# Expert rows gated on GpSimd, and added to x by accumulating transfers

## The reference

```python
sh1, sc1, gt1, sh2, sc2, gt2 = ada_mod(cond, lp['w_ada'], lp['b_ada'])   # cond: c for latent, c_ctx for context tokens
...
h2 = rms_norm(x, lp['norm2_g']) * (1.0 + sc2) + sh2
x = x + gt2 * hier_moe(h2, lp)      # 16 experts (1024 -> 512 -> 1024), two for each token, weights in combine
...
y = rms_norm(x, final_g)
```

## Time and profile before

| | us |
|---|---|
| median of 3 runs | 749.33 |
| lowest and highest | 747.24, 749.91 |
| the profiled execution, its own time | 750.44 |
| its span | 748.7 |
| busy: TensorE, VectorE | 704.5 (94%), 534.5 (71%) |
| busy: ScalarE, GpSimd | 411.4 (55%), 109.7 (15%) |

### The profile page before, as it was taken

How to read it: one execution, slowest core, us unless ns; L and a number is a source line. 1 busy time by engine, 2 the same in 40 slices (tenths; PEclk the granted TensorE clock), 3 DMA queues, 4 the chain that set the end, 5 groups by cost and what they waited for, 6 DMA issues and landing times.

```text
span 748.7 us, 10728 instructions
## 1 busy us (share of the span) xinstructions
PE 704.5 (94%) x3842; PEld 533.3 (71%) x3842; DVE 534.5 (71%) x837; ACT 411.4 (55%) x623; POOL 109.7 (15%) x166
## 2 busy tenths in 40 slices
PE   6699999989999999999999289999999999999994
PEld 2268898949977895555544278888888888888863
DVE  4363616289632035666656889999999999999997
ACT  4762532241232134545543467888888888778933
POOL 3000000000031027654221101111111111111000
PEclk9999999999999999999999589999999999999998
DMA  8991135032389609900029888999999999999663
GB/s 324 415 394 44 60 165 197 1 132 108 142 200 291 240 17 383 264 2 29 6 97 350 277 322 303 362 371 380 374 380 401 376 386 399 354 389 394 238 242 144
DMA packets 81506, 186.26 MB, mean 249 GB/s; under 512 B 9156, under 2 KB 19684, under 8 KB 78260
## 3 DMA queue, kind: packets, MB, share of 16 engines
q1 hardware_dynamic: 73252, 166.64, 60.9%
q0 software_dynamic: 6448, 16.86, 6.6%
q10 hardware_dynamic: 1760, 2.17, 1.0%
HBM read 173.16 MB, written 18.38 MB: 256 GB/s over the span
## 4 chain that ended last, share of the span: by engine, by line
PE 84%; DVE 7%; DMA 4%; ACT 2%; issue 1%; SPq 1%; POOLq 0%; DVEq 0%; ACTq 0%
PE bank L2072 56%; PE bank L1965 13%; PE bank L1974 6%; DMA slot<-in_w_ada 4%; PE bank L1985 2%; PE bank L2234 2%; PE bank L2212 1%; PE bank L2205 1%; DVE WL L1769 1%; PE bank L2035 1%; DVE big L1903 1%; DVE big L1913 1%; DVE big L1908 1%; DVE big L1843 1%; SPq L654 1%
## 5 line engine op out<-in xcount | busy, mean ns | idle before, releaser
L1769 DVE TENSOR_TENSOR WL<-slot,WH 128x1024 fp32r<-128x1024 f32 x188 | 219.2, 1220 | 9.5 <-ACT WH L1222 8.4
L1222 ACT CAST WH<-slot 128x1024 fp32r<-128x1024 f32 x188 | 183.4, 1057 | 1.4 <-PE bank L2072 1.4
L2072 PE MATMUL bank<-WH,xgTh 128*128 128x512 f32 x256 | 102.4, 400 | 3.1 <-DVE xgTl L1761 3.1
L2072 PE MATMUL bank<-WH,xgTl 128*128 128x512 f32 x256 | 100.7, 393 | 0.0
L2072 PE MATMUL bank<-hTh,WP 128*128 128x384 f32 (+1 forms) x320 | 100.0, 312 | 0.0
L2072 PE MATMUL bank<-hTh,WL 128*128 128x384 f32 (+1 forms) x320 | 98.7, 308 | 0.0
L2072 PE MATMUL bank<-hTl,WP 128*128 128x384 f32 (+1 forms) x320 | 98.7, 308 | 0.0
L2072 PE MATMUL bank<-WL,xgTh 128*128 128x512 f32 x248 | 96.5, 389 | 0.0
L1965 PE MATMUL bank<-slot,big 128*128 128x512 f32 (+1 forms) x224 | 87.7, 539 | 0.1
L1974 PE MATMUL bank<-ident,big 128*128 128x128 f32 x424 | 60.7, 284 | 7.0 <-DMA big<-h_scratch,big 5.1
L1965 PEld LDWEIGHTS bank<-slot,big 128*128 128x128 f32 x224 | 40.9, 190 | 35.1 <-issue 33.1
(11 more groups left out here) (283 smaller groups left out, 1076.5 us busy)
## 6 DMA issues: line engine op xcount, KB each, us to landing
slot<-in_w_down SPq DMA_DIRECT2D x16, 2048.0 KB, 16.7
slot<-in_w_up SPq DMA_DIRECT2D x15, 2048.0 KB, 17.7
slot<-in_w_gate SPq DMA_DIRECT2D x13, 2048.0 KB, 17.6
slot<-in_w_ada SPq DMA_DIRECT2D x12, 2048.0 KB, 11.1
slot<-in_w_in SPq DMA_DIRECT2D x6, 2048.0 KB, 22.4
y_scratch<-dftp SPq DMA_DIRECT2D x1, 5120.0 KB, 35.7
big<-y_scratch SPq DMA_DIRECT2D x10, 512.0 KB, 7.4
slot<-in_w_out SPq DMA_DIRECT2D x2, 2048.0 KB, 15.1
```

The costliest lines, as they stand in the source:

```text
L1222: act.copy(WH[:, high_half(w, s), r, :], quarter(n, s, w, r)).then_inc(high_ok[w], 1)
L1769: dve.tensor_tensor(quarter_low(n, s, w, r), quarter(n, s, w, r), WH[:, high_half(w, s), r, :].bitcast(F32), ALU.subtract).then_inc(low_ok ...
L2072: ins = pe.matmul(out, l[u], r[v], start=first and i == 0, stop=last and i == 2)
```

## The change

Six edits:

1. **GpSimd gates rows ahead of the scatter.** `gate_of` builds, for each of the 128 slots of an expert, its gate row: two comparisons of the token number with 511.5, then in two halves of 512 columns context gate x side, latent gate x side, and their sum. `scatter` multiplies the expert's 128 x 1024 results by it. Step m is now gate_of(m - 1), gather(m + 2), scatter(m - 1).
2. **The last two experts** get their gate rows behind the last scatter (`last_gate`). VectorE multiplies their banks by them (`last_gated`); `kept_high` copies that, `kept_low` subtracts.
3. **Accumulating transfers.** SP's ten loads go. GpSimd issues five transfers that add the first table to x in SBUF, then, each behind its own tile's first, five that add the second.
4. **The end.** TensorE's identity products go; it runs the last rows of slot 0 for tiles 0 to 2, then slot 1's, then tiles 3 and 4. VectorE adds the two banks to x and norms.
5. **x is kept.** SP stores x to `x1_scratch`, five transfers of 512 KB (for the branch that isn't taken): three ahead of the first expert weights, one behind gt2, one ahead of the load of expert 2's up weights.
6. **Places.** `fg` moves to the end of the loop, `gate_row` takes its place; VectorE's `keep_rows` copies two columns instead of one.

```diff
-SUM_BANKS = [(2, 3), (4, 7), (5, 6), (2, 3), (4, 7)]
+SUM_BANKS = [(2, 3), (4, 7), (5, 6), (0, 1), (2, 3)]
+SUMS_AHEAD = 3
...
+            for b in range(NT - 2):
+                sp.wait_ge(wt2_ok, ADDED[("wa", b, 1)])
+                keep_x1(b)
             full(sp, "o", NT - 2)
...
+            sp.wait_ge(x1_ok, 2)
+            keep_x1(NT - 1)
             load_weights(1, 2, 0, 1)
...
-            def load_results():
-                table = y_dram.rearrange("(k t p) n -> p t k n", k=2, p=P)
-                for t in range(NT):
-                    for k in range(2):
-                        sp.dma_start(yab[:, t, k], table[:, t, k]).then_inc(yab_in[t][k], 16)
...
-            def scatter(n, s):
+            def gate_rows(n, tokens, out):
+
+                for c, op in enumerate((ALU.is_lt, ALU.is_gt)):
+                    ins = pool.tensor_scalar(side[:, c:c + 1], tokens, LAT - 0.5, None, op)
+                ins.then_inc(side_ok, 1)
+                pool.wait_ge(side_ok, n + 1)
+                pool.sem_inc(gather_go, 1)
+                for h in range(2):
+                    half = slice(h * 512, (h + 1) * 512)
+                    if h == 1:
+                        pool.wait_ge(gate_ok, 2 * n + 1)
+                        pool.sem_inc(gather_go, 1)
+                    pool.tensor_scalar(other_gate, gt2[:, 1, half], side[:, 1:2], None, ALU.mult)
+                    pool.tensor_scalar(out[:, half], gt2[:, 0, half], side[:, 0:1], None, ALU.mult).then_inc(gate_part, 1)
+                    pool.wait_ge(gate_part, 2 * n + h + 1)
+                    pool.sem_inc(gather_go, 1)
+                    pool.tensor_tensor(out[:, half], out[:, half], other_gate, ALU.add).then_inc(gate_ok, 1)
+
+            def gate_of(n, s):
 
                 pool.wait_ge(sidx_ok, n + 1)
+                wait_past(pool, y_gated, n)
+                pool.sem_inc(gather_go, 1)
+                gate_rows(n, kept_rows[:, s, 0:1], gate_row)
+
+            def scatter(n, s, gated=True):
+
                 pool.wait_ge(y_cp, n + 1)
+                if gated:
+                    pool.wait_ge(gate_ok, 2 * n + 2)
+                    pool.sem_inc(gather_go, 1)
+                    pool.tensor_tensor(yout[:, s, :], yout[:, s, :], gate_row, ALU.mult).then_inc(y_gated, 1)
...
+                if m != 0 and not kept(p, m):
+                    gate_of(n - 1, 1 - s)
                 if m is None or m + 2 < NE:
                     gather(n + 2, s)
                 if m != 0 and not kept(p, m):
                     scatter(n - 1, 1 - s)
+
+            def add_results(again):
+
+                table = y_dram.rearrange("(k t p) n -> p k t n", k=2, p=P)
+                for t in range(NT):
+                    pool.dma_start(x[:, t, :], table[:, 0, t], accum_op=ALU.add).then_inc(results_added[t], 16)
+                for t in range(NT):
+                    pool.wait_ge(results_added[t], 32 * again + 16)
+                    pool.dma_start(x[:, t, :], table[:, 1, t], accum_op=ALU.add).then_inc(results_added[t], 16)
             pool.wait_ge(table_zero, 16)
             one_pass(0)
+            pool.wait_ge(used[0], (NE - 1) * 4)
+            pool.wait_ge(idx_ok, NE)
+            for s in range(KEPT):
+                gate_rows(NE - KEPT + s, idx[:, s, 0:1], last_gate[:, s, :])
+            pool.wait_ge(x1_out, 16 * NT)
+            for s in range(2):
+                pool.wait_ge(y_out[s], (pairs - 1) * 16)
+            add_results(0)
...
+                    act.wait_ge(last_y_ok, 2 * s + h + 1)
+                    act.copy(yH[s][:, h * 512:(h + 1) * 512], last_y[s][:, h * 512:(h + 1) * 512]).then_inc(yH_ok, 1)
...
+                    last_gated(0)
+                    selection(1)
                     kept_low(0)
-                    selection(1)
-                    for t in range(NT - 1):
-                        both_results(t)
+                    last_gated(1)
                     kept_low(1)
...
+                    dve.scalar_tensor_tensor(out=last_y[s][:, half], in0=kept_bank(s, h), scalar=1.0 / W_SCALE,
+                                             in1=last_gate[:, s, half], op0=ALU.mult, op1=ALU.mult).then_inc(last_y_ok, 1)
...
             def added(t, again):
+                dve.wait_ge(results_added[t], 32 * again + 32)
                 for h in range(2):
                     half = slice(h * 512, (h + 1) * 512)
                     dve.wait_ge(f_sum, 2 * (again * NT + t) + h + 1)
+                    dve.tensor_tensor(x[:, t, half], x[:, t, half], bank[SUM_BANKS[t][h]][:, :], ALU.add).then_inc(x_final, 1)
...
             def final(again):
                 for t in range(NT):
-                    gated(t, again)
                     added(t, again)
-                    if t == 0 and again == 0:
-                        both_results(NT - 1)
-                    elif t > 0:
+                    if t > 0:
                         final_norm(t - 1, again)
                 final_norm(NT - 1, again)
...
+                pe.wait_ge(last_y_ok, 2)
+                for s in range(KEPT):
+                    for t in range(SUMS_AHEAD):
+                        rows_added(t, s)
+                for t in range(SUMS_AHEAD, NT):
+                    if t == SUMS_AHEAD:
+                        pe.wait_ge(last_y_ok, 2 * KEPT)
+                    else:
+                        pe.wait_ge(x_final, 2 * (again * NT) + 2)
                     for s in range(KEPT):
+                        rows_added(t, s)
```

More of the change, by code:

```diff
@@ L929, in _ @@
                 for t in range(NT):
-                    for k in range(2):
-                        pool.wait_ge(yab_in[t][k], 16)
+                    pool.wait_ge(results_added[t], 32)
                 pool.wait_ge(f_sum, 2 * NT)
                 for s in range(2):
-                    scatter(NE - 2 + s, s)
+                    scatter(NE - 2 + s, s, False)
                 for s in range(2):
@@ L938, in _ @@
                     one_pass(p)
+                pool.wait_ge(x_back, 16)
+                add_results(1)
                 pool.sem_inc(stores_ok, 1)
@@ L1828, in selection, with last_gated @@
                 link(dve.tensor_copy(last_tok[:, s:s + 1], idx[:, s, 0:1]))
-                dve.wait_ge(tail_in, 4 * 16)
+                dve.wait_ge(tail_in, 2 * 16)
                 dve.tensor_scalar(selT[s][:, :], toks, last_tok[:, s:s + 1], None, ALU.is_equal).then_inc(selT_ok, 1)
+            def last_gated(s):
+                n = NE - KEPT + s
+                dve.wait_ge(gate_ok, 2 * n + 2)
+                dve.wait_ge(used[2], n * 4 + 4)
+                for h in range(2):
+                    half = slice(h * 512, (h + 1) * 512)
+                    dve.scalar_tensor_tensor(out=last_y[s][:, half], in0=kept_bank(s, h), scalar=1.0 / W_SCALE,
+                                             in1=last_gate[:, s, half], op0=ALU.mult, op1=ALU.mult).then_inc(last_y_ok, 1)
             def kept_low(s):
@@ L1836, in kept_low @@
                     dve.wait_ge(yH_ok, 2 * s + h + 1)
-                    dve.scalar_tensor_tensor(out=yL[s][:, half], in0=kept_bank(s, h), scalar=1.0 / W_SCALE,
-                                             in1=yH[s][:, half].bitcast(F32), op0=ALU.mult, op1=ALU.subtract).then_inc(yL_ok, 1)
-            def both_results(t):
-                for k in range(2):
-                    dve.wait_ge(yab_in[t][k], 16)
-                dve.tensor_tensor(yab[:, t, 0], yab[:, t, 0], yab[:, t, 1], ALU.add).then_inc(both_ok, 1)
+                    dve.tensor_tensor(yL[s][:, half], last_y[s][:, half], yH[s][:, half].bitcast(F32), ALU.subtract)\
+                       .then_inc(yL_ok, 1)
             def rest_of_routing():
@@ L1898, in one_pass, with added @@
                 expert_steps(dve, p, step)
-            def gated(t, again):
+            def added(t, again):
+                dve.wait_ge(results_added[t], 32 * again + 32)
                 for h in range(2):
@@ L1937, in _ @@
                 for s in range(KEPT):
-                    dve.tensor_scalar(selT[s][:, :], x[:, 0, 0:TOK], 0.0, None, ALU.mult)
+                    dve.tensor_scalar(selT[s][:, :], gt2[:, 0, 0:TOK], 0.0, None, ALU.mult)
                     for y in (yH[s], yL[s]):
-                        dve.tensor_scalar(y[:, :], x[:, 0, :], 0.0, None, ALU.mult)
-                for t in range(NT):
-                    for k in range(2):
-                        dve.wait_ge(yab_in[t][k], 32)
-                for t in range(NT):
-                    ins = dve.tensor_tensor(yab[:, t, 0], yab[:, t, 0], yab[:, t, 1], ALU.add)
+                        ins = dve.tensor_scalar(y[:, :], gt2[:, 0, :], 0.0, None, ALU.mult)
                 ins.then_inc(selT_ok, 1)
+                dve.wait_ge(tail_in, 3 * 16)
                 final(1)
```

85 lines of the change are left out of this document (43 added, 42 removed).

## The result

The changed kernel takes 824.5 us (median of 5 runs, 823.7 to 825.9) against 749.9 (5 runs, 747.2 to 750.2): a ratio of 1.0999, 95% interval 1.0985 to 1.1013. The forecast was 815, its range 780 to 852, slower. The profiled execution took 824.69 with a span of 822.9; the one of before 750.44 with 748.7.

A forecast was written before the change was run, and what follows sets the result against it. The prediction took TensorE as full at 17.83 us per expert, with VectorE and DMA within 3%. It summed 750.44 + 57.5 (loop) + 8 (tail) = 815.9, less 1.1 for the median: 815 us, range 780 to 852.

The forecast's parts named there:

- The loop: Expert loop: VectorE held 4.6 us per expert, period 21.94, TensorE +4.1 per expert, +57.5 us over 14 experts.
- two meetings in the attention stage: L1553 against L860, at 398.79 and 299.99: VectorE stood still, the engines taking turns, one instruction each.
- 80% of 2.11: Expert loop: the product ahead of the scatter holds VectorE 2.11 us, with 80% of VectorE's work taken as locking.
- A tensor_scalar at 0.60 us: GpSimd's gate rows: each 512-column tensor_scalar priced at 0.60 us from the one-input COPY L815, upper end 1.27.
- 7.3 us in a 14.8 us hole, for GpSimd itself hidden: Expert loop: GpSimd's added work, 7.3 us per expert, fits its 14.8 us wait and costs GpSimd nothing.
- The upper bound of the range: Expert loop with tensor_scalar at 1.27 us: +6.2 per expert, +87; with +14 in the tail, 852 us.
- the 832 for a hold by whole instructions: Expert loop: lock held for whole instructions, each costing g, 5.8 us per expert, result 832.
- The tail: After the last scatter: gate rows and accumulating transfers delay tile 0 to 737.5, end 752.9 against 745.13, +8 us.
- The new end's own worth: Tail: without identity products and their sums the end comes at 739.7 instead of 745.13, -5.4 us if undisturbed.
- Rival 2: No exclusion in the loop, accumulation at half the rate: tile 0 whole at 730.9, 750 us, no change; chance 0.04.
- Rivals 1 and 3: Loop: first, no exclusion or work fits gaps, 744 us, chance 0.07; second, GpSimd enters only at run ends, 785, 0.12.
- Rival 4: Expert loop: GpSimd becomes the bound, 25.6 us per expert, gather late, TensorE waits for rows, 867 us; chance 0.08.

The follow-up runs named there:

- no_last_gates: Changed kernel without the expert loop's gate rows and product, the last two experts multiplied by the latent gate instead of gate rows: 748.4 us, ratio 0.998.
- copies: Changed kernel with the loop's gate rows and products replaced by 12 GpSimd SBUF-to-SBUF copies of 128x1024 per expert: 872.2 us.

## Why the prediction was right

**The loop.** Forecast 4.6 us held per expert, a period of 21.94 and +57.5; measured 4.71 and 22.05. The last scatter was forecast 59.9 late, 57.5 by the loop and 2.4 by its own product, and is 59.4 late when counted from the gather for expert 2. The mechanism was right: VectorE is held while GpSimd reads SBUF, and TensorE waits for its low parts. The rule taken from two meetings in the attention stage, one instruction of GpSimd between two of VectorE, is what L941 and L944 show. It didn't foresee that a copy with one input is held like the rest. Within the sum two errors cancelled: the product held 2.3 to 2.5 us where 80% of 2.11 was put down, the gates 2.2 where it was 2.9; in the expert shown one of two sums lies beside reads of banks and holds nothing.

**A tensor_scalar at 0.60 us was wrong.** It takes 1.57. That came from a one-input COPY; the two-input 1.27, my upper end, was still too low. So "7.3 us in a 14.8 us hole, for GpSimd itself hidden" failed: with its own waits for VectorE, GpSimd is busy for 91% of the 22 us. The loop's time did not suffer, since the extra length of a tensor_scalar holds VectorE little: 0.41 at most, where I had 0.38. That the two agree is luck. By the prediction's own rule, that an operation of g costs g - 0.22, one of 1.57 would hold 1.35; with that the sum is 0.8 x (4 x 1.35 + 2.10 + 2.11) = 7.7 us per expert and 858 in all, outside the range. The price was wrong and the rule was wrong for this operation, and the two cancelled. What sets how much of an operation holds stays open: nearly all of a product, two thirds of a copy, about a quarter of a tensor_scalar at most. The upper bound of the range, which let all of 1.27 hold, was too pessimistic for that reason, and so was the 832 for a hold by whole instructions.

**The tail** was forecast at +8, of which 2.4 is the scatter's delay, so +5.4 behind the scatter. It is +16.5. That is where the forecast is most off. Two terms of it were mis-sized. The last gate rows took from the scatter's start 28.2 us to the first transfer, forecast 22 (21 and the issue). The eight tensor_scalar took 17.7 in place of 12.2; the comparisons, 1.8, and the gaps between instructions, 1.4, had been put at nothing; the four sums took 6.1 in place of 8.8. And the accumulation was put at 1.5 times a plain transfer, 1.9 us; it is 2.48, close to my bound of 2.56, and tile 0 came 18.8 instead of 13.5 us behind the first issue. Six transfers at that rate explain 3.5 of this; the other 1.8 is the start and the landing, put at 2 and 3.9 by what is left of 18.8. Those are 28.2 - 22 = +6.2 and 18.8 - 13.5 = +5.3, 11.5 together. From tile 0 to the end 15.4 was forecast and 15.0 measured, which leaves the 11.1 that are missing, so the new order of additions and norms does what was said. TensorE's end was put 5 us later for the gate rows; it came at 775.5, 55.1 later than before, so no later than the loop made it.

**The new end's own worth**, 5.4 us if nothing disturbs it, is hardly there: 1.7 in no_last_gates, since the arrival of tile 0 leads even then. Rival 2, accumulation at half the rate, was right in its rate and fell with its other half: it needed a loop without exclusion.

**Rivals 1 and 3** fall: 1 with the loop; 3, GpSimd let in only at the end of a run, because the product at 689.34 gets in at a run's start and the L923 at 697.68 in the middle of one. **Rival 4** fell short: the gather does come right behind the gates, and yet VectorE is never idle for it, and where the chain had room the period stayed. Its clock did drop a little, to 0.95 in the window, and with TensorE waiting for VectorE anyway that is no cost seen here.

Of the signs named, one came out otherwise: the DMA share was expected at 0.8 and is 0.91, though the GB/s fell to 317, 0.85 of before. No run shows why.

## What to carry to other kernels

Before work goes to a GpSimd that looks idle, count the operations there that read SBUF against VectorE's with two SBUF inputs and its copies from SBUF to SBUF: each such meeting costs VectorE time although its own instruction list is unchanged, and a VectorE at 97% has none to give. Take an operation's price from the same operation, not from one with the same number of inputs, and where it stands ahead of a transfer that the end waits for, price the chain. An accumulating transfer saves VectorE's addition and costs the DMA engines twice the time: here that gained 1 us for tiles whose arrival isn't waited for, and cost time where the end waited for the first of them.

## What the runs showed of the hardware

- GpSimd's tensor_scalar of 128x512 takes 1.50 us by a constant and 1.57 by a column, more than a two-input tensor_tensor of the same size (1.26 to 1.28). It holds VectorE for at most 0.41 us of that; a 128x1024 copy, 1.04 alone, for 0.68 on average; a 1024-wide product of 2.4 to 2.5 for 2.2 to 2.5, all or nearly all of it; a fill of 0.96 for nothing.
- Held are VectorE's operations with two SBUF inputs (L1832 at 1519 ns in place of 1220) and its copies with one (20 columns, 2.39 us in place of 0.17), not one that reads a bank (L1837 at 678 ns in copies).
- Being held shows as duration, not as a wait: a 20-column COPY lasts 2.39 us, and no view names GpSimd as its releaser.
- Accumulating transfers run at 211 GB/s with full engines against 413 plain, and their issue takes GpSimd 0.86 us against 0.53.
